# A second pair of score banks and three transpose banks in the third attention of a two-block model

## The reference, cut to what matters

```python
def nsa_attention(q, kc, vc, ks, vs, kw, vw, gates, rel_bias):
    """q (B,S,H,D); kc,vc (B,Ncmp,Hkv,D); ks,vs,kw,vw (B,S,Hkv,D); gates (B,S,H,3)."""
    ...
        s_s = jnp.einsum('bqhgd,bhqnkd->bhgqnk', qc, k_sel).astype(jnp.float32)
        s_s = s_s + jnp.moveaxis(bias_s, -1, 2)
        p_s = masked_softmax(...)
        o_s = jnp.einsum('bhgqnk,bhqnkd->bqhgd', p_s.astype(v_sel.dtype), v_sel)
        ...
        s_w = jnp.einsum('bqhgd,bkhd->bhgqk', qc, kwc).astype(jnp.float32) + head_bias(dist_w)
        p_w = masked_softmax(s_w, mask_w)
        o_w = jnp.einsum('bhgqk,bkhd->bqhgd', p_w.astype(vwc.dtype), vwc)
        return gc[..., 0:1] * o_c + gc[..., 1:2] * o_s + gc[..., 2:3] * o_w
```

## Time and profile before

| | |
|---|---|
| runs | 2223.79 us median of 3 (2222.8 to 2226.46) |
| profiled execution | 2226.47 us |
| its span, first to last instruction | 2224.7 us |
| PE busy | 2183.1 us, 98% of the span |
| DVE busy | 1276.9 us, 57% |
| ACT busy | 945.7 us, 43% |
| mean granted clock of PE | 0.994 of full speed |
| third attention, first scores to first product of the output projection | 1662.4 to 1754.0 us |

### The profile page before, as it was taken

The page is one execution under the profiler, slowest core; times in us unless marked ns, Lnnn a source line. Parts: engine busy times, 40 slices in busy tenths (PEclk is TensorE's granted clock), DMA queues, the critical chain, the costliest instruction groups (busy, mean ns, idle before and its releaser), DMA issues.

```text
span 2224.7 us, 25927 instructions
## 1 busy us (share of the span) xinstructions
PE 2183.1 (98%) x10008; PEld 1711.2 (77%) x10008; DVE 1276.9 (57%) x2198; ACT 945.7 (43%) x1558; POOL 804.4 (36%) x315
## 2 busy tenths in 40 slices
PE   8999999999999999999999999999999999999998
PEld 5777788888887767667888888887774688888887
DVE  6887665553258688773665562176967643333224
ACT  6676443333233566663344332233237532222224
POOL 1232444444443222113444444433330144444432
PEclk9999999999999999999999999999999999999999
DMA  8211333333222211112233333244310133233222
GB/s 281 67 58 53 93 95 98 102 95 104 95 93 78 72 48 39 39 33 90 96 99 95 95 105 103 90 125 165 112 60 11 38 95 95 95 99 109 91 100 85
DMA packets 58650, 199.97 MB, mean 90 GB/s; under 512 B 6720, under 2 KB 10320, under 8 KB 58528
## 3 DMA queue, kind: packets, MB, share of 16 engines
q1 hardware_dynamic: 57584, 196.21, 27.5%
q10 hardware_dynamic: 944, 2.11, 0.3%
HBM read 196.15 MB, written 7.38 MB: 91 GB/s over the span
## 4 chain that ended last, share of the span: by engine, by line
PE 88%; DVE 7%; ACT 2%; issue 1%; DMA 1%; POOL 0%; SPq 0%; DVEq 0%; ACTq 0%
PE lin L535 24%; PE lin L537 24%; PE lin L536 24%; PE obank L869 1%; PE scores L847 1%; PE turn L668 1%; PE scores L851 1%; PE stat L674 1%; PE scores L1070 1%; PE lin L586 1%; PE obank L748 1%; PE lin L588 1%; PE lin L587 1%; PE scores L705 1%; PE obank L1046 1%
## 5 line engine op out<-in xcount | busy, mean ns | idle before, releaser
L2540 POOL TENSOR_TENSOR w_lo<-slots,w_hi 128x1024 fp32r<-128x1024 f32 (+4 forms) x309 | 801.5, 2596 | 1395.9 <-ACT w_hi L2021 1395.9
L2021 ACT ACTIVATE w_hi<-slots 128x1024 fp32r<-128x1024 f32 (+4 forms) x312 | 347.0, 1113 | 576.9 <-DMA slots<-in_w_ffn_in 281.0
L535 PE MATMUL lin<-g_hi,w_hi 128*128 128x512 f32 x1400 | 550.0, 393 | 0.0
L537 PE MATMUL lin<-g_hi,w_lo 128*128 128x512 f32 x1400 | 545.0, 389 | 0.0
L536 PE MATMUL lin<-g_lo,w_hi 128*128 128x512 f32 x1400 | 544.9, 389 | 0.0
L535 PEld LDWEIGHTS lin<-g_hi,w_hi 128*128 128x128 f32 x1400 | 262.8, 188 | 59.3 <-issue 5.0
L536 PEld LDWEIGHTS lin<-g_lo,w_hi 128*128 128x128 f32 x1400 | 262.8, 188 | 55.8 <-issue 1.7
L537 PEld LDWEIGHTS lin<-g_hi,w_lo 128*128 128x128 f32 x1400 | 262.7, 188 | 54.7
L1255 DVE TENSOR_TENSOR h<-lin,h 128x512 f32<-128x512 f32 x72 | 49.7, 690 | 306.1 <-PE lin L537 296.9
L536 PE MATMUL lin<-f_lo,w_hi 128*128 128x512 f32 x528 | 205.4, 389 | 0.0
L535 PE MATMUL lin<-f_hi,w_hi 128*128 128x512 f32 x528 | 205.4, 389 | 0.0
(11 more groups left out here) (479 smaller groups left out, 3526.9 us busy)
## 6 DMA issues: line engine op xcount, KB each, us to landing
slots<-in_w_ffn_in SPq DMA_DIRECT2D x132, 512.0 KB, 3.5
slots<-in_w_ffn_out SPq DMA_DIRECT2D x48, 704.0 KB, 4.0
slots<-in_w_ple SPq DMA_DIRECT2D x24, 640.0 KB, 3.8
slots<-in_w_a_qkv SPq DMA_DIRECT2D x24, 512.0 KB, 3.6
slots<-in_w_c_in SPq DMA_DIRECT2D x21, 512.0 KB, 3.6
slots<-in_w_b_wo SPq DMA_DIRECT2D x16, 512.0 KB, 3.5
slots<-in_w_b_pair SPq DMA_DIRECT2D x8, 768.0 KB, 4.2
slots<-in_w_a_wo SPq DMA_DIRECT2D x16, 256.0 KB, 2.6
```

The costliest lines, as they stand in the source:

```text
L535: pe.matmul(bank[:, parity, :], hi, x_hi, start=k == 0, stop=False)
L537: mm = pe.matmul(bank[:, parity, :], lo, x_hi, start=False, stop=k == len(rhs) - 1)
L2021: ac.activation(w_hi[:, slot, at_], slots[:, slot, at_], ACT.Copy).then_inc(q.hi_made, 1)
L2540: po.tensor_tensor(w_lo[:, slot, at_], slots[:, slot, at_], w_hi[:, slot, at_].bitcast(F32), ALU.subtract).then_inc(q.weights_split, 1)
```

## The change

The scores get a second pair of banks: units with odd n from 3 on use `stat` (x=0) and `lin[:, 1]` (x=1), the others `scores`. `score` now waits for the bias of unit n-2 instead of n-1 (for n=3 it waits for the second `gl_log` and the last projection tile instead, which free the two new banks). The transposes lose `lin[:, 1]` and go round three banks, `turn[:, 0]`, `turn[:, 1]` and `lin[:, 0]`, one bank after the other by 2n+x; the transposes of number m wait for the copy of number m-3, where before they waited for that of m-4. `inv_sqrt` of the second half moves on ACT from the head of s=1 to behind the exponentials of (0, 2), ahead of those of (0, 3). The order of the lists is otherwise as before.

```diff
-        turns = (turn, lin)
+        turned_banks = (turn[:, 0, :], turn[:, 1, :], lin[:, 0, :])
+
+        def score_bank(n, x):
+
+            return (stat[:, :], lin[:, 1, :])[x] if n > 2 and n % 2 else scores[:, x, :]
...
             def score(s, k):
                 i = NQ - 1 - k
-                wait(pe, q.c_biased, 8 * s + 2 * k)
+                n = 4 * s + k
+                if n == 3:
+                    pe.wait_ge(q.gl_log, 2)
+                    pe.wait_ge(q.tile_taken, TILE["c_in"] + len(C_IN))
+                else:
+                    wait(pe, q.c_biased, 2 * n if n < 3 else 2 * n - 2)
                 for kv in range(2):
                     rows = slice(64 * kv, 64 * kv + 64)
-                    mm = pe.matmul(scores[:, kv, 0:LEN[i]], c_z[rows, s // 2, i * P:(i + 1) * P],
+                    mm = pe.matmul(score_bank(n, kv)[:, 0:LEN[i]], c_z[rows, s // 2, i * P:(i + 1) * P],
                                    c_z[rows, 4 + s % 2, 0:LEN[i]], start=True, stop=True)
                 mm.then_inc(q.c_scored, 1)
...
                         for x in range(2):
-                            wait(pe, q.c_tcopied, 2 * n - 3 + x)
-                            turn_weights(sc(s - 1, i, x), i, turns[n % 2][:, x, :]).then_inc(q.c_turned, 1)
+                            wait(pe, q.c_tcopied, 2 * n + x - 2)
+                            turn_weights(sc(s - 1, i, x), i, turned_banks[(2 * n + x) % 3]).then_inc(q.c_turned, 1)
...
-                    ve.tensor_tensor_reduce(out=sc(s, i, x), in0=scores[:, x, 0:LEN[i]],
+                    ve.tensor_tensor_reduce(out=sc(s, i, x), in0=score_bank(n, x)[:, 0:LEN[i]],
...
             for s in range(CH + 1):
-                if s == 1:
-                    inv_sqrt(gl_e[:, 1, :], GV, q.gl_ss, q.gl_log, q.gl_fac, 2, 2)
...
                     if s < CH and 4 * s + k > 1:
                         exps(s, k)
+                    if s == 0 and k == 2:
+                        inv_sqrt(gl_e[:, 1, :], GV, q.gl_ss, q.gl_log, q.gl_fac, 2, 2)
...
-                                          turns[k % 2][:, x, 0:LEN[i]].rearrange("p (j c) -> p j c", c=P), ACT.Copy)\
+                                          turned_banks[(8 * (s - 1) + 2 * k + x) % 3][:, 0:LEN[i]]
+                                          .rearrange("p (j c) -> p j c", c=P), ACT.Copy)\
                                 .then_inc(q.c_tcopied, 1)
```

## The result

The changed kernel takes 2262.08 us (median of 4 runs, 2260.0 to 2268.91) against 2223.3 us (median of 4, 2221.51 to 2226.46) for the kernel before: +38.8 us, a ratio of 1.0178 [1.0154, 1.0203]. The forecast was 2257, +33, in a range of 2241 to 2279. The profiled execution took 2262.51 us, with a span of 2260.8; PE is busy 97% of it and the mean granted clock is 0.989 (it was 0.994).

A forecast was written before the change was run, and what follows sets the result against it. The prediction took heads s=2 to 6 as bound by PE's own work and the stage's start by a chain over DVE and ACT. Terms 7.0 + 19.7 + 2.2 + 4.1 = +33.0 gave 2257 us, range 2241 to 2279.

The forecast's parts named there:

- The ring (Part 1): Heads s=2 to 6: transposes wait for ACT's copy in a PE-DVE-ACT loop, 13.40 or 13.71 us a head; +19.7 us.
- The lower clock in the heads: Head 2: PE's lower clock may last from the start; half of 4.4 taken, +2.2 us, bounds 0 and 4.4.
- the clock falls again and again: Rival, heads 3 to 7: PE's clock keeps dropping; half the time down adds 11 to 14 us; 2264 to 2285; chance 0.28.
- the low ends: Low side, 2243 us: copy-to-PE hops 5.4 us less in all, start +4.2, head 2's clock term 0.
- the high ends: High side, 2264 us: start +7.5, head 2's clock term 4.4, and 2 us for the copy-to-PE hops.
- The start (Part 3): Stage start up to scores (2,0): earlier root delays scores (0,3) by 1.4 us; +7.0 us taken, bounds +4.2 to +7.5.
- the 3.2 us wait: Stage start: PE idles from 1679.1 to 1682.3 for the copies (0,0), and its clock falls there.
- The second score pair (Part 2): Scores in heads s=2 to 6 no longer wait for DVE; gain between 0 and 0.8 us, taken as 0.
- Head 7 and the rest: Head 7's first three rounds take 10.89 us against 6.81, +4.1; its last round and what follows unchanged.
- faster: Rival: scores run ahead of DVE, stall before 1681.33 filled, clock stays up; 2219 us; needs copies before exponentials; chance 0.06.

The follow-up runs named there:

- experiment 7: Changed kernel, PE making the scores a second time between the two sets of transposes in all rounds but k=0: 2258.6 us, ratio 1.0151.
- experiment 2: Kernel before with only the transposes changed to three banks; scores, their wait and the root as before: 2259.68 us, ratio 1.0162.
- experiment 5: Changed kernel with only ACT's copy x=0 of (s-1,k) moved ahead of the exponentials (s,k): 2224.91 us, ratio 1.0002.
- experiment 6: Changed kernel, PE making the scores a second time between the two sets of transposes in every round: 2262.38 us, ratio 1.0169.
- experiment 9: Changed kernel, both copies before exponentials, second score pair from n=5, root a round later, normalisations and a rounding moved to later heads: 2225.45 us, ratio 1.0000.
- experiment 3: Kernel before (four transpose banks, one score pair) with both ACT copies ahead of the exponentials: 2224.86 us, ratio 1.0001.
- experiment 1: Changed kernel with both ACT copies of (s-1,k) ahead of the exponentials (s,k): 2222.55 us, ratio 0.9991.

## Why the prediction was right, and where its sizes were off

**The ring (Part 1): right, and to a few hundredths.** In head 6 the rounds are 4.45, 3.66, 2.89 and 2.55 us (1754.12, 1758.57, 1762.23, 1765.12, 1767.67); the prediction had 4.39, 3.61, 2.89 and 2.51. Its pieces are a little less good than their sum. The copies of that head, in the timeline (start us, us):

```profile
1757.39 0.57 ACT L2486 ACTIVATE g<-turn 128x512 f32<-128x512 f32 x1
...
1758.02 0.55 PE L673 MATMUL turn<-consts,arena 128*128 128x128 f32 x3 [1.35 <-ACT g L2486]
```

Scores to exponentials is 1.85 and exponentials to copy 1.42 (1755.97 to 1757.39), both as taken from the earlier trace rows. Copy to PE is 0.63, not the 0.72 of the earlier trace rows; why it was longer there is not shown (the pair of copies at 1679.63, shown further down, lets PE start after 0.63 too). Transposes to scores is 0.55, not 0.40. The two errors nearly cancel. The last round with the extra product is 2.82 us in head 3 of experiment 7 (scores at 1721.30 and 1724.12), as predicted. With heads of 13.55 and 13.81 us at the full clock (experiment 7's head 3 for the second) the five would take 3 x 13.55 + 2 x 13.81 = 68.3 us, against 67.6 predicted: a term of +20.3 instead of +19.7. Experiments 2 and 5 show that it is this ring and no other: three banks bring it, and the one copy that closes it, made earlier, takes it away.

**The lower clock in the heads: right in kind, the size was off.** This is the term that was mis-sized. I took +2.2, half of head 2 at the lower level; the five heads take 74.98 us, 6.7 above the 68.3 just worked out. The clock came back in head 2, as I had it, but fell again three times, near 1704, 1721 and 1738 us. Stretches of the changed kernel, before a fall and in it:

```profile
1698.00:1704.00 6.00, 4.01 (x22) 1.53 (x21) 3.66 (x16) 3.15 (x11) 0.00 (x0) 1.00 0.00 1
1704.00:1710.00 6.00, 5.68 (x21) 2.92 (x21) 1.64 (x9) 2.78 (x10) 0.00 (x0) 0.50 0.01 3
1711.00:1721.00 10.00, 6.73 (x42) 3.00 (x40) 5.60 (x27) 6.21 (x19) 0.00 (x0) 1.00 0.00 0
1722.00:1727.00 5.00, 5.00 (x16) 2.37 (x16) 1.24 (x2) 0.07 (x1) 0.00 (x0) 0.50 0.00 0
1728.00:1738.00 10.00, 6.84 (x42) 3.22 (x40) 5.56 (x27) 6.21 (x21) 0.00 (x0) 1.00 0.00 0
1739.00:1741.00 2.00, 2.00 (x6) 0.51 (x4) 0.00 (x0) 0.00 (x0) 0.00 (x0) 0.50 0.00 0
1742.00:1767.00 25.00, 17.30 (x100) 7.56 (x96) 14.67 (x65) 14.63 (x48) 0.00 (x0) 1.00 0.00 1
```

That is the rival "the clock falls again and again": a stretch with PE busy some two thirds, then a fall; at the lower level PE is nearly full, and the clock rises again. It is the rival's mechanism at under half of its price: 4.5 us beyond the 2.2 of the forecast, where the rival had 11 to 14 or more, since from 1742 on, at 17.30 of 25.00 us busy, the clock stayed up. So the measured time lies near the top of the forecast's own range (2243 to 2264), where the rival's begins. That range was added up wrongly: from 33.0 the low ends (5.4, 2.8 and 2.2 less) give +22.6 and the high ends (0.5, 2.2 and 2.0 more) +37.7, which on the median of 2223.79 is 2246 to 2261.5. The measured +38.8 lies 1.1 above that, and it is this term that took it there: term by term the 33.0 became 8.0 + 20.3 + 6.7 + 3.8. The rule by which the prediction held the rival down, from the Trainium skill (TensorE: Matmul & The Clock Gate, section "Why this matters for your kernels"), names long idle gaps between bursts as what to avoid; here PE waited at most 1.35 us at a time for the copies in these heads, and the clock fell all the same, so the measurement decides against reading it as the only way in. Experiments 6 and 7 show that work in the gaps keeps the clock up most of the time (0.99 over the five heads of experiment 6, and 1.00, 0.99 and 1.00 in heads 3, 4 and 6 of experiment 7, but 0.90 in its head 5). Why it fell in heads 2, 3 and 4 and not in 5 and 6, at much the same share of PE work, stays open.

**The start (Part 3): +7.0 predicted, +8.0 measured: right in kind, 0.5 above its upper bound of +7.5.** The logarithm and the scores (0,3) after the change, then the copies (0,0) and the transposes that wait for them:

```profile
1672.57 0.67 ACT L2085 ACTIVATE arena<-stat,eps 128x512 f32<-128x512 f32 x1
...
1673.29 0.58 PE L1080 MATMUL stat<-arena 64*128 64x128 f32 x1 [2.23 <-ACT arena L2085]
...
1679.63 1.06 ACT L2486 ACTIVATE arena<-turn 128x512 f32<-128x512 f32 x2
1680.26 0.90 PE L673 MATMUL turn<-consts,sinb 128*128 128x128 f32 x3 [2.35 <-ACT arena L2486]
```

The scores (0,3) start 2.87 us after the scores (0,2), before it was 1.52 (1674.81): 1.35 later, predicted 1.4. What I had not seen is that PE's wait there, 2.23 us instead of 0.88, is itself followed by the lower clock (0.50 from 1674 to 1676), ahead of the 3.2 us wait to which I had put the fall; that second wait is 2.35. The copies (0,0) that end it come 9.21 us after the scores (0,2) (1670.42 to 1679.63), before it was 7.32 (1673.29 to 1680.61): 1.9 later, where the prediction had 1.0. Experiment 2 splits the 8.0 us: 6.1 are the ring's, 1.9 those of the earlier root. The lower clock at the start was seen with and without the change; only experiment 9 kept it away there, and met it in the heads.

**The second score pair (Part 2): +0 predicted, and shown.** The wait of the scores for DVE is gone, as said, and buys nothing: experiment 2 is as slow without it, and experiment 3 as fast without it as experiment 1 with it.

**Head 7 and the rest: +4.1 predicted, +3.8 measured.** What lies before and behind the stage did not change beyond what one execution differs from another (the work before it was 2.9 us shorter in the profile of after, which is why the span grew by 36.1 us and the stage by 38.9).

**The rival "faster" named the right condition, but not its worth.** It said that the copy (s-1,k) would have to be made before the exponentials (s,k). Made so, the ring is gone (experiments 1 and 5), yet the time is that of the kernel before, not 2219: in heads 2 to 6 PE was already full, and the start's gap, clock and all, stayed.

## What to carry to other kernels

Before a buffer is taken from a rotation, walk the new wait through every list in which it stands: a copy that sits behind other work of the same round in one engine's order closes a ring, and its length can be added up from the durations of the old profile. The cure can then be the order of the engine that empties the buffers, not another buffer: here one copy per round made before the exponentials was worth all of the 38.8 us. And where PE is about to go from full to two thirds busy, weigh the lower clock in every pass, not in the first one only.

## What the hardware showed that I had not expected

In the heads the granted clock fell to 0.50 three times though no wait of PE for a copy was longer than 1.35 us: PE had been busy 4.01 of 6.00, 6.73 of 10.00 and 6.84 of 10.00 us ahead of the falls, and at 17.30 of 25.00 us it did not fall. With the same ring and the gaps filled by scores that nobody reads, it was 0.99 over the five heads, and those were 2.4 us shorter (72.55 against 74.98) although PE did 80 matmuls more; the whole time was the same (2262.38 us against 2262.08).
